# Attention scores with the rotated half paired across the array's rows, and a split list of entry loads, in a three-block network kernel

## The reference, cut to what matters

```python
k_r = jnp.broadcast_to(k_rope[:, :, None, :], (B, S, N_ATTN_HEADS, QK_ROPE_DIM))
k = jnp.concatenate([k_nope, k_r], axis=-1)
q = rms_norm(q, q_head_g)
k = rms_norm(k, k_head_g)
q = jnp.concatenate([q[..., :QK_NOPE_DIM], apply_rope(q[..., QK_NOPE_DIM:], cos, sin)], axis=-1)
k = jnp.concatenate([k[..., :QK_NOPE_DIM], apply_rope(k[..., QK_NOPE_DIM:], cos, sin)], axis=-1)
...
s = jnp.einsum('bhqd,bhkd->bhqk', q_blk, kt, preferred_element_type=jnp.float32) * scale
p = jax.nn.softmax(s, axis=-1).astype(vt.dtype)
return jnp.einsum('bhqk,bhkd->bhqd', p, vt)
```

## Time and profile before

| | before |
|---|---|
| median of 3 runs | 4653.86 us (4651.34 to 4656.09) |
| the profiled execution | 4654.69 us |
| its span, first to last instruction | 4652.8 us |
| PE busy | 4291.7 us (92%) |
| DVE busy | 1533.8 us (33%) |
| ACT busy | 821.1 us (18%) |
| POOL busy | 270.7 us (6%) |
| mean granted PE clock | 0.968 |

### The profile page before, as it was taken

One profiled execution on the slowest core, in us unless ns is written; L12 is line 12 of the kernel. 1 busy time (PEld: TensorE's weight loads), 2 busy tenths in 40 slices (PEclk: granted clock), 3 DMA queues, 4 the chain that ended last, 5 costly groups with the idle time before them and its releaser, 6 DMA issues. The chain is left out here.

```text
span 4652.8 us, 33591 instructions
## 1 busy us (share of the span) xinstructions
PE 4291.7 (92%) x13320; PEld 2167.9 (47%) x13320; DVE 1533.8 (33%) x2091; ACT 821.1 (18%) x1566; POOL 270.7 (6%) x262
## 2 busy tenths in 40 slices
PE   4999986999997999986999997998998899999899
PEld 2444452444443444452444443445986444444344
DVE  4787422111111785422111112544454211111001
ACT  1143311101102143311101102322221100000000
POOL 0000000000000000000000000002552000000000
PEclk9999987999998999987999998999999999999999
DMA  6300118999994000118999993110001111111210
GB/s 221 115 37 0 58 72 298 360 346 342 360 325 153 0 37 0 52 77 298 359 347 342 360 328 110 40 32 10 19 1 59 50 36 36 36 38 34 91 54 32
DMA packets 251870, 647.48 MB, mean 139 GB/s; under 512 B 16336, under 2 KB 102992, under 8 KB 251728
## 3 DMA queue, kind: packets, MB, share of 16 engines
q1 hardware_dynamic: 242512, 611.95, 36.6%
q0 software_dynamic: 9216, 33.56, 3.0%
HBM read 603.51 MB, written 41.94 MB: 139 GB/s over the span
## 5 line engine op out<-in xcount | busy, mean ns | idle before, releaser
L1404 PE MATMUL ps<-w_ring,h_act 128*128 128x512 f32 x3072 | 1334.0, 595 | 19.7 <-ACT h_act L1481 13.7
L1404 PEld LDWEIGHTS ps<-w_ring,h_act 128*128 128x128 f32 x3072 | 581.5, 190 | 744.2 <-issue 716.1
L2651 PE MATMUL ps<-h_act,w_up 128*128 128x512 f32 x1408 | 607.0, 594 | 7.8 <-DMA w_up<-in_ffn_w_up 7.8
L2651 PEld LDWEIGHTS ps<-h_act,w_up 128*128 128x128 f32 x1408 | 268.4, 191 | 345.8 <-issue 337.8
L2733 PE MATMUL ps<-w_down,ffn_hidden 128*128 128x512 f32 x704 | 304.9, 596 | 17.5 <-DMA w_down<-in_ffn_w_down 17.5
L835 DVE SCALAR_TENSOR_TENSOR y<-y,par_one 128x1024 f32<-128x1024 f32 x240 | 307.5, 1281 | 3.9
L1499 DVE SCALAR_TENSOR_TENSOR h_act<-ps,gate,gate_row 128x1024 f32<-128x1024 f32 x32 | 41.1, 1284 | 775.2 <-PE ps L1404 775.2
L1469 ACT ACTIVATE h_act<-ps 128x1024 f32<-128x1024 f32 x32 | 32.8, 1025 | 1181.9 <-PE ps L1404 1181.9
L1723 PE MATMUL ps<-h_act,arena_two 128*128 128x512 f32 x544 | 235.1, 592 | 1.9 <-DVE h_act L369 1.0
L521 PE MATMUL ps<-h_act,arena_a 128*128 128x512 f32 x512 | 221.6, 593 | 5.8 <-DVE h_act L369 2.0
L2733 PEld LDWEIGHTS ps<-w_down,ffn_hidden 128*128 128x128 f32 x704 | 134.6, 191 | 187.8 <-issue 169.5
(11 more groups left out here) (369 smaller groups left out, 4389.2 us busy)
## 6 DMA issues: line engine op xcount, KB each, us to landing
w_ring<-in_w_gate SPq DMA_DIRECT2D x128, 1024.0 KB, 8.4
w_ring<-in_w_up SPq DMA_DIRECT2D x128, 1024.0 KB, 7.1
w_ring<-in_w_down SPq DMA_DIRECT2D x128, 1024.0 KB, 5.3
w_mod<-in_w_ada SPq DMA_DIRECT2D x48, 512.0 KB, 6.0
w_mod<-in_w_mod SPq DMA_DIRECT2D x48, 512.0 KB, 6.5
w_up<-in_ffn_w_up SPq DMA_DIRECT2D x44, 512.0 KB, 4.9
arena_b<-in_w_ada SPq DMA_DIRECT2D x32, 512.0 KB, 4.4
w_down<-in_ffn_w_down SPq DMA_DIRECT2D x22, 512.0 KB, 8.8
```

The lines of the kernel that those rows point to most:

```text
L1404: last = nc.tensor.matmul(ps[:, bank + i, :], lhs[:, k * P:(k + 1) * P], ring[:, c, k % kp, i * HALF:(i + 1) * HALF], start=(k == 0), stop ...
L2651: last = nc.tensor.matmul(ps[:, 4 * b + 2 * a + half, :], ws[:, b, a, k, :], core.h[:, k, half * HALF:(half + 1) * HALF], start=(k == 0), ...
```

## The change

The rotated keys get a tile of their own, `krT` (named k_rope in the rows): keys 0 to 511 on partitions 0 to 63, keys 512 to 1023 on partitions 64 to 127, for each head. The rotated queries are written twice, once for each partition half. `scores(u)` then makes both 128-row products first and behind them two 64-row products, on rows 0 to 63 into the bank of the first key half, on rows 64 to 127 into that of the second.

To get both key halves into one transpose, preparation takes the tiles in the order 0, 4, 1, 5, 2, 6, 3, 7 (`PREP`), and after every second tile a fourth group of transposes (KR_TURN) turns the scaled rotated keys of a pair of tiles; VectorE copies it to `krT` (`keep_k_rope`). TensorE waits for krT_kept ahead of scores(0). `load_entry` is cut in two: with `first` true it issues x and the first two pieces of w_in and returns; the rest is issued by a second call at the head of SP's list in `mix_one`. In layer 1 both calls stand there one behind the other.

```diff
+PREP = [t + i * QT // 2 for t in range(QT // 2) for i in range(2)]
+Q_TURN, ROPE_TURN, K_TURN, KR_TURN = range(4)
+TURNS = [(n, kind) for n in range(QT) for kind in ((Q_TURN, ROPE_TURN, K_TURN, KR_TURN) if n % 2 else (Q_TURN, ROPE_TURN, K_TURN))]
...
-def load_entry(sp, core, ar, a, l, x_in, sems):
+def load_entry(sp, core, ar, a, l, x_in, sems, first):
...
+    if first:
+        for t in range(4):
+            rows(t)
+        conv(0, c0)
+        for t in range(4, QT):
+            rows(t)
+        return
     conv(1, c1)
     sp.dma_start(ar.w_in[:, :, 0:LAT], w_k[:, :, 0:LAT]).then_inc(lat, 16)
     conv(2, c2)
...
-    tok_r = take(3, 2 * HEADS * ROPE)
+    tok_qr, tok_kr = take(3, HEADS, NH, ROPE), take(2, HEADS, NH, ROPE)
...
+        krT = sb("k_rope", [P, HEADS, HALF])
...
                 if not loaded_before:
-                    load_entry(sp, core, ar, a, l, x_in, entry)
+                    load_entry(sp, core, ar, a, l, x_in, entry, True)
+                load_entry(sp, core, ar, a, l, x_in, entry, False)
...
+                    if n >= 2:
+                        turn_heads(n - 2, K_TURN)
+                        if n % 2:
+                            turn_heads(n - 2, KR_TURN)
...
-                    rows = slice((m % 2) * ROPE, (m % 2 + 1) * ROPE)
                     for i in range(NH):
-                        cols = slice(i * HALF, (i + 1) * HALF)
-                        out = ps[:, 2 * (u % 2) + i, :]
-                        nc.tensor.matmul(out, h[:, m, t * P:(t + 1) * P], kT[:, m, cols], start=True, stop=False)
-                        last = nc.tensor.matmul(out, h[rows, 4 + m // 2, t * P:(t + 1) * P], h[rows, 6 + m // 2, cols],
+                        nc.tensor.matmul(ps[:, 2 * (u % 2) + i, :], h[:, m, t * P:(t + 1) * P], kT[:, m, i * HALF:(i + 1) * HALF],
+                                         start=True, stop=False)
+                    for i in range(NH):
+                        rows = slice(i * ROPE, (i + 1) * ROPE)
+                        last = nc.tensor.matmul(ps[:, 2 * (u % 2) + i, :], h[rows, 4 + m, t * P:(t + 1) * P], krT[rows, m, :],
                                                 start=False, stop=True)
...
+                pe.wait_ge(krT_kept, QT // 2)
...
-                    nc.vector.tensor_tensor(dest[:, :, 0:hr], part[0][:, :, 0:hr], part[1][:, :, hr:], ALU.subtract).then_inc(q_turned_rope, 1)
-                    nc.vector.tensor_tensor(dest[:, :, hr:], part[0][:, :, hr:], part[1][:, :, 0:hr], ALU.add).then_inc(q_turned_rope, 1)
+                    nc.vector.tensor_tensor(tok_qr[:, c, :, :, 0:hr], low[0], high[1], ALU.subtract).then_inc(q_turned_rope, 1)
+                    nc.vector.tensor_tensor(tok_qr[:, c, :, :, hr:], high[0], low[1], ALU.add).then_inc(q_turned_rope, 1)
...
+                def keep_k_rope(j):
+                    dve.wait_ge(head_turned, turns_to(2 * j + 1, KR_TURN))
+                    nc.vector.tensor_copy(krT[:, :, j * P:(j + 1) * P],
+                                          ps[:, turn_bank(2 * j + 1, KR_TURN), :].rearrange("p (m n) -> p m n", m=4)).then_inc(krT_kept, 1)
...
+                    if n >= 3 and n % 2:
+                        keep_k_rope(n // 2 - 1)
```

More of the change, by code:

```diff
@@ L589, in free, with product @@
                         pe.wait_ge(q_kept, t + 1)
[L591 to L595, removed]
+                def product(n, i):
+                    free(4 * n + i)
+                    cols = slice(PREP[n] * P, (PREP[n] + 1) * P)
+                    out = ps[:, ring[(4 * n + i) % len(ring)], :]
                     if i in (V_, K_):
@@ L622, in turn_heads @@
                     for m in range(4):
-                        last = nc.tensor.transpose(ps[:, 6 + n % 2, m * P:(m + 1) * P], src[:, m * P:(m + 1) * P], core.c("ident", P))
+                        last = nc.tensor.transpose(ps[:, turn_bank(n, kind), m * P:(m + 1) * P], src[:, m * P:(m + 1) * P],
+                                                   core.c("ident", P))
                     last.then_inc(head_turned, 1)
[L626 to L639, removed]
+                for n in range(QT + 2):
+                    if n < QT:
+                        product(n, V_)
+                        product(n, K_)
+                    if n >= 2:
+                        turn_heads(n - 2, Q_TURN)
+                    if n < QT:
+                        product(n, R_)
+                    if n >= 2:
+                        turn_heads(n - 2, ROPE_TURN)
+                    if n < QT:
+                        product(n, Q_)
+                    if n >= 2:
+                        turn_heads(n - 2, K_TURN)
+                        if n % 2:
+                            turn_heads(n - 2, KR_TURN)
@@ new lines, in turn_q_rope, with keep_rope @@
+                    both = [P, HEADS, NH, hr]
+                    low = [part[i][:, :, 0:hr].unsqueeze(2).to_broadcast(both) for i in range(2)]
+                    high = [part[i][:, :, hr:].unsqueeze(2).to_broadcast(both) for i in range(2)]
+                    nc.vector.tensor_tensor(tok_qr[:, c, :, :, 0:hr], low[0], high[1], ALU.subtract).then_inc(q_turned_rope, 1)
+                    nc.vector.tensor_tensor(tok_qr[:, c, :, :, hr:], high[0], low[1], ALU.add).then_inc(q_turned_rope, 1)
+                def keep_rope(n):
+                    t = PREP[n]
+                    dve.wait_ge(head_turned, turns_to(n, ROPE_TURN))
+                    nc.vector.tensor_copy(h[:, 4:8, t * P:(t + 1) * P],
+                                          ps[:, turn_bank(n, ROPE_TURN), :].rearrange("p (m n) -> p m n", m=4)).then_inc(ropeT_kept, 1)
@@ L2809, in block_one @@
                 first = modulation_of(core, a, 0, (0, 1), [core.h[:, i, :] for i in range(6)], [core.h[:, 6 + i, :] for i in range(2)], sems)
-                begin(core, a, first, lambda sp: load_entry(sp, core, ar, a, 0, x_in, entry))
+                begin(core, a, first, lambda sp: load_entry(sp, core, ar, a, 0, x_in, entry, True))
             sems = held.enter_context(stage(nc, *Modulation.names(4)))
```

173 lines of the change are left out of this document (90 added, 83 removed).

## The result

| | before | after |
|---|---|---|
| median | 4654.98 us (4651.34 to 4656.38, 4 runs) | 4582.07 us (4580.88 to 4582.57, 4 runs) |
| span of the profiled execution | 4652.8 us | 4580.3 us |

The ratio is 0.9844, with a 95% interval of 0.9827 to 0.9861: the kernel became 72.9 us faster. The forecast was 4579 us in a range of 4568 to 4603.

A forecast was written before the change was run, and what follows sets the result against it. TensorE, busy 92% of the span, was taken as the bound. Attention 60.2 less preparation 5.2 plus start 19.9 gave 74.9 us saved, about 4579 us for the median, range 4568 to 4603.

The forecast's parts named there:

- Preparation: Stage before attention: added transposes and VectorE copies cost 2.6 us a layer, 5.2 in all; bounds 3.8 and 13.
- the start: Begin of layer 0: barrier lifts at 40.6 instead of 60.53 us, 19.9 us saved; bounds 0 and 19.9.
- attention: Attention of both layers: 60.2 us saved, from shorter units and first scores that end sooner.
- Scores: Attention unit on TensorE: 0.39 us less from fewer changes, 0.86 from full overlap; 6.81 becomes 5.56.
- strict order: Rival in scores: program order allows only three slots, unit 5.99 us, total saving 54, time 4600; chance 0.10.
- no overlap: Rival in scores: 64-row products adding onto open sums do not overlap, unit 6.42 us, time 4624; chance 0.04.
- Loads: Layer 0's load_entry: barrier waits for SP's issuing, so moving later loads saves 19.9 us; no new wait.
- Which engine sets the pace: Attention intervals: VectorE holds 12 at 6.16 us (layer 0), three at 4.83 (layer 1); others 5.56; saves 26.3 and 31.4.
- the upper bound of 13: Preparation, both layers: cost in us if all of VectorE's added work is laid bare.
- The slower rival: Attention: TensorE idling in VectorE-bound units drops the clock to 1.2 GHz, +5.5 us a unit; chance 0.02.
- one of the signs by which the forecast would have been wrong: Attention: a granted clock below 1 between the first and last scores.
- the 14 units: Slower rival in attention: from 14 of the 64 units at half clock, the loss beats the gain.

The follow-up runs named there:

- two runs: Changed kernel with scores' products in the old order, 4644.14 us; changed kernel with both 64-row products on rows 0 to 63, 4620.92 us.
- its repeat: The changed kernel as it is, run once more beside other runs as their yardstick: 4581.14 us, ratio 0.9844.

## Why the prediction was right, and where it was not

The total came within 3 us, and part of that is luck. Preparation was charged 8.4 us too little and the start credited 1.5 too much; against that stood 3.8 more in attention and 3.6 in stretches that the forecast put at nothing.

**Scores.** Right. The unit is 5.56 us as forecast, in both of its parts (0.39 and 0.86, shown apart by two runs). The overlap could be read from L1746 although it lay in another stage, with other operands and with products that open their banks. The rivals of strict order (5.99) and of no overlap (6.42) are out: the 64-row group takes 1.06 us, and its matmuls start in pairs. In the code both matmuls of the lower half stand ahead of those of the upper; which row of the trace belongs to which half it does not say. In L1746 the code has four of one half ahead of four of the other, and all eight took 1.92 us. The Trainium skill (TensorE: Matmul & The Clock Gate, Part 3, "The mechanism") says that matmuls start and end in strict program order. The traces do not agree for different row halves: by that rule the group here would have lasted 1.5 and that of L1746 over 3.0.

**Loads.** Right in mechanism and size: 19.9 forecast, 19 to 22 measured by undoing it and by doing it alone. The last x row was issued by 38.3 and not 39.3, so ScalarE started at 39.67, 20.9 us earlier than before; 18.4 of these reached preparation. The first transposes (L347) stretched over 6.58 us instead of 5.18, and the first convolution product was only 19.5 us earlier. Most of these transposes took 0.42 us each, and 0.27 later on; that this is the lower clock is argued from the two lengths, the granted clock reads 1.00 there. Another 1.0 went at the 32 tiny products ahead of preparation (L222), which took 4.65 us instead of 3.63.

**Which engine sets the pace.** Right for VectorE's 6.16 and 4.84. Two sizes were off. I counted the last interval between turns, from unit 30 to 31, at 5.56; no scores are made in it, and it is 2.59 in both kernels, so each layer gained 3.0 more than my sum. Against that stood waits of L703 for ScalarE's copies and the clock in layer 0, about 1.2 us, and in layer 1 1.0 where weigh begins.

**Preparation.** This step failed: 2.6 us a layer forecast, 6.6 to 7.0 measured. Both layers together are 13.6, just past the upper bound of 13. At the full clock it is 5.4 (55.89 against 50.44). The added transposes were charged rightly, 0.43 each. I compared VectorE's work with TensorE's period, found room, and so charged no wait inside the loop. But an average is not an order. The added group needs at once a bank that VectorE frees late, and TensorE stood still 0.95 us each time, three times a layer, and 1.5 at the end.

VectorE had room, as the forecast said: it waits for ScalarE in every step. It frees the bank late by its order, because the copy stands behind a rotation whose input is not there yet. Moving that copy ahead takes the 0.95 us waits away and two tiles from 12.84 to 12.08. Taking the keys' copy from VectorE does nothing in the loop by itself (12.83) and removes the 1.5 at the end; once the order is mended it gives the last 0.4 as well (11.67). Moving TensorE's group makes the loop longer (13.51), so the place of the wait on TensorE is not the cause.

**The slower rival.** The clock did fall in layer 0's attention, for 6.8 us in the profile of the kernel after, for 10.2 in that of its repeat, and not at all before. That was one of the signs by which the forecast would have been wrong. It happened among the units that VectorE holds; that TensorE's waits there are the reason is only argued. At half speed 6.8 us cost at most 3.4, far from the 14 units it would have needed. Over the whole span the mean granted clock was 0.968 before and 0.967 after.

**The rest.** 1.0 and 2.6 us were gained in stretches that the change does not touch. No run tells their cause. That the periods at the lower clock fall elsewhere there is only argued.

## What to carry to other kernels

Small products on half of the array's rows are worth pairing if the two stand side by side: in a unit here the overlap gave twice what the fewer changes of shape gave, and the row halves without the order gave nothing. A stage that ends at a barrier of all engines should not end with a long list of loads that only the next stage needs; issue them at the head of that next stage instead. When you add a step to a loop that alternates two banks, look up who frees the bank and what stands ahead of that on its engine; average room does not answer it. And filler work on an engine near the bound should be spread evenly, not rounded up at the start.

## What the runs showed of the hardware

- Two 64-row float32 products on different row halves run side by side even where they add onto banks that 128-row products have just opened: 1.06 us for four matmuls against 1.91 on the same rows. A 128-row product between them undoes it.
- A change between 128-row and 64-row products costs 0.2 us; the units of three kernels (6.81 with four changes, 6.42 and 5.56 with two) all fit it. The Trainium skill (TensorEngine Tiling (Array Packing), Tiling Modes, "Key Properties") says that a change of tiling mode drains the engine; the trace agrees so far as 0.2 us are lost at each change; it does not show that this is a drain.
- Loads cost the engines that do not use them: 20 us of issuing on SP held ScalarE's squares back at a barrier, although they read nothing of what those issues load.
